# A decoder step on one core: the sample's cache pages laid on 32 partitions each instead of 128

## The chip, the cores and the metric

The kernel runs on one core of one Trainium2 chip. The metric is the device time of one execution in microseconds. The engines are TensorE (PE, with its weight loads as PEld), VectorE (DVE), ScalarE (ACT), GpSimd (POOL) and SyncE (SP). A transfer between device memory and the on-chip memory of 128 partitions is cut into packets, one for each contiguous run, and the packets are moved by the core's 16 DMA engines. Transfers are issued by SP (queue q1 in the profile), by ACT (queue q10) and by POOL (queue q0); each queue keeps its own order.

## The reference

One layer of a hybrid decoder for a prompt of 1024 tokens and a sample of 8 sequences with one new token each. Every token passes an attention with a compressed cache, a retention branch, and a mixer in which each of 8 heads picks 16 of 16384 experts, whose rows of `peer_u` and `peer_v` (4 KB each) are fetched by number. The change touches only the sample's attention over its paged cache:

```
ckv_all = concatenate([cache_ckv[l][page_table].reshape(DB, past_len, KV_LORA), ckv], axis=1)
kr_all  = concatenate([cache_krope[l][page_table].reshape(DB, past_len, QK_ROPE), krope], axis=1)
s = (einsum('bqhc,bkc->bhqk', q_abs, ckv_all)
     + einsum('bqhr,bkr->bhqk', q_pe, kr_all)) * scale
p = softmax(s)
o = einsum('bhqk,bkc->bqhc', p, ckv_all)
```

A page holds 128 tokens. A token is 256 numbers of the latent (1 KB in float32) and 32 numbers of the rotary key (128 bytes). Each of the 8 sequences has 32 pages. Softmax and both sums run over all the tokens of a sequence, so that the order of the tokens is free as long as scores, probabilities and values agree on it.

## The kernel before, in words

The prompt is worked in 8 blocks of 128 tokens, then the sample as a ninth block. Beside each block's "front" (projections, attention, retention) run the "experts" of the block before: POOL gathers rows of 128 tokens at a time (512 KB a gather) into a ring of 9 slots, DVE multiplies the `u` rows with the token, and the `v` rows are added by DVE or, by way of a diagonal made by ACT, by PE. How many expert steps stand between two pieces of the front is fixed at build time, the same on all engines.

The sample's part has two stages that matter here.

- The retention stage (`dve_sample_ret`, `pe_sample`, `sp_sample`). For each of the 8 sequences SP loads a state of 512 KB into one of three buffers, DVE updates it (L2074), PE multiplies with it (L1074), and SP stores it (L684). A buffer is loaded again only when its store has landed (L678, then L652). Between these, on the same queue, SP issues one group of four pages and their rotary keys for each sequence (`load_pages`, L664 and L668). So in SP's queue stand, again and again: load of a state, four pages, four rotary keys, store of a state.
- The attention stage (`pe_sample_attention`, `act_sample_attention`, `dve_sample`). A sequence is 8 groups of four pages. For each group DVE transposes the pages and the keys in blocks of 32 by 32 (L2087, L2088), PE makes the scores with 9 pairs of matmuls (L1107), and a sequence later PE multiplies probabilities and pages (L1141). 16 places hold groups; SP refills a place when PE has used it (L662). From group 8 on the rotary keys are issued by ACT (`load_ropes`, L1623), between its own computing: exponents, the diagonals for the experts (L2254), and the queries of the next sequence (`stage_queries`, L1588 and L1590), which stand behind the loads of a whole sequence in ACT's order.

Each page number is read from the page table into a register (L659, L1617), and each page is a transfer of its own. DVE waits for the 8 transfers of a group together (L2085).

Of the kernel before, what the change touches and what calls it, by code (L numbers as in the profile page):

```python
# [19 lines left out]
ds = bass.ds  # L20
# [76 lines left out]
def program(nc, a, out, const):  # L97
    _, SEQ, D = a["x_prompt"].shape
    NB = a["x_sample"].shape[0]
    _, NPHYS, PAGE, KVL = a["cache_ckv"].shape  # L100
    ROPE = a["cache_krope"].shape[3]
# [67 lines left out]
    for t, part in order:  # L169
        for i, (name, w, c, wd) in enumerate(b for b in stream if b[0] == part):  # L170
            if shared(t, name, i):
                continue
            k = w.shape[0] // P
# [3 lines left out]
    def used_through(t, name, i):  # L177
        return sum(load_at[t, name, i])
# [4 lines left out]
    with ExitStack() as ctx:  # L183
# [3 lines left out]
        def sem(name):  # L187
            return ctx.enter_context(nc.semaphore(name))
# [302 lines left out]
        s_pages = [sem(f"s_pages{i}") for i in range(PAGE_SLOTS)]  # L491
# [130 lines left out]
        def page_at(g):  # L622
            i = g % PAGE_SLOTS
            home, i = ((KV, i) if i < NCH else (wbuf, i - NCH) if i < NCH + 4 else (z, i - NCH - 4) if i < NCH + 6
                       else (xr[T % 2], 0) if i == NCH + 6 else (uk, 0))
            return home[:, i * 4 * KVL:(i + 1) * 4 * KVL]
# [6 lines left out]
        def krope_at(g):  # L633
            i = g % PAGE_SLOTS
            if i >= 14:
                return knat[:, (i - 14) * 4 * ROPE:(i - 13) * 4 * ROPE]
            return KV[:, VAT + i * 4 * ROPE:VAT + (i + 1) * 4 * ROPE]

        def s_state_buf(b):
            at_ = VAT + NPAGES * ROPE + b % 3 * RH * RDV  # L640
            return KV[:, at_:at_ + RH * RDV]

        def sp_sample(sp):

            pv_done.wait(sp, T - 1)
            sp.wait_ge(s_gates, 16)
            DJ.wait_drained(sp, T - 1, "stateU")
            sp.dma_start(out["ret_p"][0, 0].rearrange("h d e -> d h e"),
                         state[:, :].rearrange("p (h e) -> p h e", h=RH)).then_inc(state_out, 16)

            def load_state(b):
                sp.dma_start(s_state_buf(b).rearrange("p (h e) -> p h e", h=RH),  # L652
                             a["state_ret"][0][ds(b, 1)].rearrange("o h d e -> d (o h) e")).then_inc(s_state_in[b % 3], 16)

            sp.wait_ge(table_in, 16)

            def load_pages(g):

                _, numbers = nc.values_load_multi_w_load_instructions(  # L659
                    pages_reg[0:1, 4 * g:4 * g + 4], engines=[mybir.EngineType.SP], min_val=0, max_val=NPHYS - 1)  # L660
                if g >= PAGE_SLOTS:
                    sp.wait_ge(s_pv.sem, g - PAGE_SLOTS + 1)  # L662
                for k, page in enumerate(numbers):
                    sp.dma_start(page_at(g)[:, k * KVL:(k + 1) * KVL],  # L664
                                 a["cache_ckv"][0][ds(page, 1)].rearrange("o p c -> (o p) c")).then_inc(s_pages[g % PAGE_SLOTS], 16)
                if g < NCH:
                    for k, page in enumerate(numbers):
                        sp.dma_start(krope_at(g)[:, k * ROPE:(k + 1) * ROPE],  # L668
                                     a["cache_krope"][0][ds(page, 1)].rearrange("o p c -> (o p) c")).then_inc(s_pages[g % PAGE_SLOTS], 16)

            for b in range(2):
                load_state(b)
            for b in range(NB):
                if b + 2 < NB:

                    s_oret.wait(sp, b - 1)
                    if b >= 1:
                        sp.wait_ge(s_state_stored[(b + 2) % 3], 16 * ((b + 2) // 3))  # L678
                    load_state(b + 2)
                for c in range(NCH):  # L680
                    if c * NB // NCH == b:
                        load_pages(c)
                s_state_new.wait(sp, b)
                sp.dma_start(out["ret_s"][0][b:b + 1].rearrange("o h d e -> d (o h) e"),  # L684
                             s_state_buf(b).rearrange("p (h e) -> p h e", h=RH)).then_inc(s_state_stored[b % 3], 16)
            sp.wait_ge(ckv_stored, 32 * (T + 1))
            s_masked.wait(sp, NB - 1)
            ret_squares.wait(sp, T)
            sp.dma_start(flat, out["ckv_s"][0].rearrange("b s c -> s (b c)")).then_inc(s_flat, 16)
            sp.wait_ge(w_used, used_through(T, "uq", NU - 1))  # L690
            for i in range(3):
                sp.wait_ge(s_state_stored[i], 16 * len(range(i, NB, 3)))
            sp_store_y(sp, T - 2)
            for g in range(NCH, NB * NCH):
                if g == NCH + 6:
                    sp.wait_ge(y_stored, 16 * (T - 1))
                if g == NCH + 7:
                    AS.wait_drained(sp, 0, "qabs")
                load_pages(g)
# [879 lines left out]
        def act_sample_attention(act):  # L1579
            AS.wait_drained(act, 0, "qabs")  # L1580
            act.wait_ge(s_setup, 1)

            def stage_queries(b):
                s_sc_filled.wait(act, b - 2)
                queries = qrep.rearrange("p (k h b) -> p k h b", k=9, h=NH)
                for q in range(4):
                    quarter = slice(32 * q, 32 * (q + 1))
                    nc.scalar.activation(qsc[b % 2].rearrange("p (k q m) -> p k q m", k=8, q=4)[quarter, :, q, 0:NH],  # L1588
                                         queries[quarter, 0:8, :, b], ACT.Copy)
                    last = nc.scalar.activation(qsc_rope[b % 2][quarter, 32 * q:32 * q + NH], queries[quarter, 8, :, b], ACT.Copy)  # L1590
                last.then_inc(s_staged.sem, 1)

            def exponents(b):
                s_nm.wait(act, b)
                s_pt.wait(act, b - 1)
                nc.scalar.activation(WK[:, 0:D], PS[:, scores_at(b):scores_at(b) + 2 * 512], ACT.Exp, bias=nmx[:, 0:1], scale=SCALE,
                                     accum_out=sums[:, 0:1]).then_inc(s_exp.sem, 1)
                s_diff.wait(act, b)
                nc.scalar.activation(pnew4.rearrange("p (j m) -> p j m", j=4), drow.unsqueeze(1).broadcast_to([1, 4, 32]), ACT.Exp,
                                     scale=SCALE).then_inc(s_exp.sem, 1)  # L1600

            def scaled(b):
                s_pv_new.wait(act, b)
                s_weight.wait(act, b)
                nc.scalar.activation(o_sc, bank[6][:, 0:KVL], ACT.Copy, scale=sums[:, 1:2]).then_inc(s_osc.sem, 1)

            def turned_out(b):
                s_ot_filled.wait(act, b)
                nc.scalar.activation(ota.rearrange("p (c b) -> p c b", b=NB)[:, :, b], bank[6][:, 400:400 + 2 * NH],
                                     ACT.Copy).then_inc(s_ota.sem, 1)  # L1610

            act.wait_ge(table_in, 16)

            def load_ropes(g):
                if g >= NB * NCH:
                    return
                _, numbers = nc.values_load_multi_w_load_instructions(  # L1617
                    pages_reg[0:1, 4 * g:4 * g + 4], engines=[mybir.EngineType.Activation], min_val=0, max_val=NPHYS - 1)
                s_turned.wait(act, 0, g - PAGE_SLOTS + 1)
                if g == 14:  # L1620
                    act.wait_ge(ckv_stored, 32 * (T + 1))
                for k, page in enumerate(numbers):
                    act.dma_start(krope_at(g)[:, k * ROPE:(k + 1) * ROPE],  # L1623
                                  a["cache_krope"][0][ds(page, 1)].rearrange("o p c -> (o p) c")).then_inc(s_pages[g % PAGE_SLOTS], 16)

            for i in range(3):
                act.wait_ge(s_state_stored[i], 16 * len(range(i, NB, 3)))
            stage_queries(0)
            for b in range(NB):
                for c in range(NCH):  # L1630
                    load_ropes((b + 1) * NCH + c)
                    if b > 0 and c in (1, 3, 4):
                        {1: exponents, 3: scaled, 4: turned_out}[c](b - 1)
                    if c == NCH - 1 and b + 1 < NB:
                        stage_queries(b + 1)
                    yield "page"
            for stage in (exponents, scaled, turned_out):
                stage(NB - 1)
# [692 lines left out]
PAGE_SLOTS = 16  # L2331
# [76 lines left out]
```

## Time and profile before

| | us |
|---|---|
| median of 3 runs | 4161.53 (4159.66 to 4172.78) |
| the profiled execution's own time | 4134.78 |
| its span | 4133.0 |
| PE busy | 3237.0 (78%) |
| DVE busy | 2704.7 (65%) |
| POOL busy | 2527.7 (61%) |
| ACT busy | 742.9 (18%) |
| mean rate of the DMA engines | 360 GB/s |

The profile is of one execution. All places in time below are microseconds from the start of its span. The sample's retention stage begins near 3456, its attention's first scores stand at 3604, and its last at 3925; what follows is the sample's projections and experts, up to 4133. "Packets" are counted for each queue; a queue's share is the time that its packets took as a share of the time of all 16 DMA engines.

### The profile page before, as it was taken

The numbers are of one execution on the slowest core, as the hardware profiler recorded it, in microseconds if no ns is written. First come the engines' busy times: TensorE is split into PE (matmuls) and PEld (weight loads), VectorE is DVE, ScalarE is ACT, GpSimd is POOL, SyncE is SP. The second block draws the span as 40 slices with busy tenths as digits, with TensorE's granted clock in tenths as the row PEclk, the third lists the DMA queues.
The fourth block names the chain that finished last, engine by engine and source line by source line (L and its number), as shares of the span: only waits on it lengthen the run. The fifth ranks groups of instructions, "written<-read, shape, count | busy, mean of one in ns | idle before, by whom it ended". The sixth has DMA issues, their size and how long they took to land.

```text
span 4133.0 us, 39221 instructions
## 1 busy us (share of the span) xinstructions
PE 3237.0 (78%) x11253; PEld 1588.6 (38%) x11253; DVE 2704.7 (65%) x6214; ACT 742.9 (18%) x2277; POOL 2527.7 (61%) x2069
## 2 busy tenths in 40 slices
PE   7887877876889876877988777877888777599954
PEld 3334333432344332433444233423344333366622
DVE  2156667767777568766886577756875577556554
ACT  2112111220112111211122022211122120111121
POOL 0005766777667767776667677666767677445462
PEclk9998999988999999889999999999999997799987
DMA  5668999999999999999999999999999999999996
GB/s 181 219 219 304 398 393 397 359 395 389 397 375 389 402 402 338 368 399 398 398 367 403 402 380 358 386 401 391 386 384 399 391 371 331 326 311 365 348 356 246
DMA packets 576043, 1489.93 MB, mean 360 GB/s; under 512 B 90267, under 2 KB 147236, under 8 KB 575812
## 3 DMA queue, kind: packets, MB, share of 16 engines
q0 software_dynamic: 297216, 1082.26, 68.3%
q1 hardware_dynamic: 238514, 392.77, 26.5%
q10 hardware_dynamic: 40098, 12.39, 1.3%
q8 instruction: 92, 1.51, 0.2%
q14 instruction: 123, 1.00, 0.1%
HBM read 1477.01 MB, written 10.20 MB: 360 GB/s over the span
## 4 chain that ended last, share of the span: by engine, by line
PE 36%; DMA 25%; POOL 17%; DVE 11%; issue 8%; ACT 3%; ACTq 1%; SPq 0%; POOLq 0%; DVEq 0%
DMA rows<-in_peer_v_dram,pe_id 16%; POOL rows L728 16%; PE PS L1190 12%; PE PS L823 11%; DMA rows<-in_peer_u_dram,pe_id 3%; PE PS L1107 3%; DVE rows L2148 3%; PE PS L832 2%; DMA wbuf<-in_w_out_dram 2%; PE PS L788 1%; DMA wbuf<-in_peer_w_q_dram 1%; DVE xr L2174 1%; PE PS L968 1%; PE PS L948 1%; DMA wbuf<-in_w_in_dram 1%
## 5 line engine op out<-in xcount | busy, mean ns | idle before, releaser
L728 POOL DMA_INDIRECT rows<-in_peer_u_dram,pe_id x1024 | 1259.9, 1230 | 880.0 <-DVE pe_id L1953 297.4
L1190 PE MATMUL PS<-rows,diags 128*128 128x512 f32 x2544 | 1344.0, 660 | 484.0 <-DMA rows<-in_peer_v_dram,pe_id 443.7
L728 POOL DMA_INDIRECT rows<-in_peer_v_dram,pe_id x1024 | 1248.3, 1219 | 671.6 <-DVE dots L2148 377.8
L2148 DVE CUSTOM_DVE_ANT_0 rows<-rows,px 128x1024 f32<-128x1024 f32 x1024 | 1242.0, 1223 | 525.0 <-DMA rows<-in_peer_u_dram,pe_id 520.4
L1190 PEld LDWEIGHTS PS<-rows,diags 128*128 128x128 f32 x2544 | 485.8, 206 | 1132.4 <-issue 979.2
L823 PE MATMUL PS<-wbuf,xt 128*128 128x512 f32 (+1 forms) x1696 | 780.4, 595 | 73.5 <-DMA wbuf<-in_w_in_dram 31.3
L2174 DVE SCALAR_TENSOR_TENSOR xr<-rows,gcoef,xr 128x1024 f32<-128x1024 f32 x388 | 498.3, 1284 | 149.1 <-issue 135.4
L823 PEld LDWEIGHTS PS<-wbuf,xt 128*128 128x128 f32 x1696 | 320.1, 196 | 494.3 <-issue 347.2
L823 PE MATMUL PS<-wbuf,wide 128*128 128x512 f32 (+1 forms) x736 | 341.6, 606 | 35.2 <-ACT wide L1301 14.8
L2254 ACT ACTIVATE diags<-ident,gcoef 128x128 f32<-128x128 f32 x636 | 231.4, 399 | 218.6 <-PE PS L1190 100.6
L823 PEld LDWEIGHTS PS<-wbuf,wide 128*128 128x128 f32 x736 | 143.6, 200 | 215.9 <-issue 162.5
L788 PE MATMUL PS<-ident,WK 128*128 128x128 f32 x572 | 96.0, 311 | 91.3 <-DVE WK L1867 47.7
L832 PE MATMUL PS<-wbuf,KV 128*128 128x512 f32 (+1 forms) x352 | 156.0, 565 | 0.0
L788 PEld LDWEIGHTS PS<-ident,WK 128*128 128x128 f32 x572 | 78.4, 161 | 139.2 <-DVE WK L1867 56.1
L1290 ACT ACTIVATE z<-PS 128x512 f32<-128x512 f32 (+1 forms) x60 | 32.8, 567 | 469.9 <-PE PS L823 210.6
L968 PE MATMUL PS<-KV,WK 128*128 128x64 f32 x576 | 81.9, 290 | 29.9 <-ACT WK L1445 29.9
L1290 ACT ACTIVATE WK<-PS 128x512 f32<-128x512 f32 x42 | 25.1, 597 | 429.9 <-PE PS L823 280.0
L948 PE MATMUL PS<-KV,qt 96*128 96x512 f32 (+3 forms) x192 | 79.6, 525 | 27.3 <-DVE mx L1816 25.7
L832 PEld LDWEIGHTS PS<-wbuf,KV 128*128 128x128 f32 x352 | 65.7, 190 | 77.2 <-issue 77.2
L968 PEld LDWEIGHTS PS<-KV,WK 128*128 128x128 f32 x576 | 73.0, 200 | 45.9 <-ACT WK L1445 40.2
L1440 ACT ACTIVATE WK<-WK,nmx 128x128 f32<-128x128 f32 (+7 forms) x64 | 49.5, 774 | 206.3 <-DVE nmx L1820 206.3
L1859 DVE TENSOR_TENSOR xr<-PS,xr 128x512 f32<-128x512 f32 x16 | 11.1, 692 | 113.8 <-PE PS L823 113.8
(375 smaller groups left out, 2682.0 us busy)
## 6 DMA issues: line engine op xcount, KB each, us to landing
wbuf<-in_w_in_dram SPq DMA_DIRECT2D x274, 512.0 KB, 10.1
wbuf<-in_peer_w_q_dram SPq DMA_DIRECT2D x134, 512.0 KB, 12.1
wbuf<-in_w_ob_dram SPq DMA_DIRECT2D x66, 512.0 KB, 8.5
wbuf<-in_w_out_dram SPq DMA_DIRECT2D x66, 512.0 KB, 11.1
wbuf<-in_w_oa_dram SPq DMA_DIRECT2D x36, 512.0 KB, 8.1
rows<-in_peer_u_dram,pe_id POOLq DMA_INDIRECT x1028, 9.3
rows<-in_peer_v_dram,pe_id POOLq DMA_INDIRECT x1024, 9.3
KV<-in_cache_ckv_dram SPq DMA_DIRECT2D x128, 128.0 KB
```

The source lines that it names most:

```text
L728: pool.indirect_dma_start(row_slot(kind, n), None, a["peer_u" if kind == "u" else "peer_v"][0], bass.IndirectOffsetOnAxis(ap=pe_id[t % 2][ ...
L788: last = nc.tensor.transpose(b[0:m, k * n:(k + 1) * n], src, ident[0:n, 0:n])
L823: last = nc.tensor.matmul(bnk, lhs[:, (k0 + j) * P:(k0 + j + 1) * P], block_w[:, j * wd:(j + 1) * wd], start=(k0 + j == 0), stop=(n == n0 ...
L832: last = nc.tensor.matmul(other, next_lhs(t, k0 + j), block_w[:, j * wd:(j + 1) * wd], start=(k0 + j == 0), stop=(n == n0 + slots - 1 and ...
L948: last = nc.tensor.matmul(DD.bank(tj, "score", h)[:, i:i + w], qt[0:HD, h * P:(h + 1) * P], key_t[0:HD, h, i:i + w], start=True, stop=True)
L968: last = nc.tensor.matmul(bank[6][:, h * VH:(h + 1) * VH], pt[:, k * P:(k + 1) * P], value[:, k, h * VH:(h + 1) * VH], start=(k == 0), sto ...
L1107: last = nc.tensor.matmul(PS[:, at_:at_ + P], qsc[b % 2][:, k * P:(k + 1) * P] if k < 8 else qsc_rope[b % 2], blocks_of[:, k] if k < 8 els ...
L1190: last = nc.tensor.matmul(bank[3 + 4 * c], diag(n), row_slot("v", n)[:, c * 512:(c + 1) * 512], start=start, stop=stop)
L1290: return nc.scalar.activation(dst[:, at_:at_ + wd], b[:, 0:wd], func, scale=scale)
L2148: V.tensor_tensor_reduce(out=row, in0=row, in1=px[:, :], scale=1.0, scalar=0.0, op0=ALU.mult, op1=ALU.add, accum_out=dots[:, at_:at_ + 1]) ...
L2174: V.scalar_tensor_tensor(out=y[:, :], in0=row_slot("v", n), scalar=gcoef[:, g % 2 * TOPK + k:g % 2 * TOPK + k + 1], in1=y[:, :], op0=ALU.m ...
L2254: nc.scalar.activation(diag(n), ident[:, :], ACT.Copy, scale=gcoef[:, g % 2 * TOPK + k:g % 2 * TOPK + k + 1]).then_inc(diag_ready.sem, 1)
```

## The change

Where four pages of a group stood beside each other along the free axis of all 128 partitions (page k in columns k * 256 to (k + 1) * 256, a token to a partition), now page k stands in partitions 32k to 32k + 31, and each partition holds four neighbouring tokens of it in its 1024 columns. The rotary keys are laid in the same way. The tiles, their size, the transposes, the matmuls, the waits and the number and order of all instructions are as before; each transfer names 32 rows of 4 KB in place of 128 rows of 1 KB (keys: 32 rows of 512 bytes in place of 128 of 128 bytes).

```
@@ load_pages, issued by SP @@
                 for k, page in enumerate(numbers):
-                    sp.dma_start(page_at(g)[:, k * KVL:(k + 1) * KVL],
-                                 a["cache_ckv"][0][ds(page, 1)].rearrange("o p c -> (o p) c")).then_inc(s_pages[g % PAGE_SLOTS], 16)
+                    sp.dma_start(page_at(g)[32 * k:32 * (k + 1), :],
+                                 a["cache_ckv"][0][ds(page, 1)].rearrange("o (p s) c -> (o p) (s c)", s=4)).then_inc(s_pages[g % PAGE_SLOTS], 16)
                 if g < NCH:
                     for k, page in enumerate(numbers):
-                        sp.dma_start(krope_at(g)[:, k * ROPE:(k + 1) * ROPE],
-                                     a["cache_krope"][0][ds(page, 1)].rearrange("o p c -> (o p) c")).then_inc(s_pages[g % PAGE_SLOTS], 16)
+                        sp.dma_start(krope_at(g)[32 * k:32 * (k + 1), :],
+                                     a["cache_krope"][0][ds(page, 1)].rearrange("o (p s) c -> (o p) (s c)", s=4)).then_inc(s_pages[g % PAGE_SLOTS], 16)
@@ load_ropes, issued by ACT @@
                 for k, page in enumerate(numbers):
-                    act.dma_start(krope_at(g)[:, k * ROPE:(k + 1) * ROPE],
-                                  a["cache_krope"][0][ds(page, 1)].rearrange("o p c -> (o p) c")).then_inc(s_pages[g % PAGE_SLOTS], 16)
+                    act.dma_start(krope_at(g)[32 * k:32 * (k + 1), :],
+                                  a["cache_krope"][0][ds(page, 1)].rearrange("o (p s) c -> (o p) (s c)", s=4)).then_inc(s_pages[g % PAGE_SLOTS], 16)
```

## Rows read from the trace of the kernel before

**Rows 1.** Stretches: from:to, length, busy us of engines, clock, DMA share, GB/s

```profile
3456.00:3565.00 109.00, 70.48 (x246) 32.55 (x246) 72.15 (x150) 7.55 (x28) 58.46 (x49) 0.76 0.93 327
...
3650.00:3900.00 250.00, 241.98 (x1687) 170.68 (x1686) 159.23 (x295) 41.39 (x137) 124.28 (x110) 0.99 1.02 345
```

**Rows 2.** Waits of PE, 3600 to 3925: us in total, times, longest

```profile
PE PS L1107 <- ACT knat L1590: 6.2, 1, 6.2
...
PE PS L1190 <- DMA rows<-in_peer_v_dram,pe_id: 3.3, 1, 3.3
```

**Rows 3.** Waits of SP, 3650 to 3900

```profile
SPq L664 <- PE PS L1141: 89.2, 6, 31.6
```

**Rows 4.** Waits of POOL, 3650 to 3900

```profile
POOL rows L728 <- DVE dots L2148: 103.8, 26, 11.0
```

**Rows 5.** Chain that ended last, retention stage: start us, us, what

```profile
3494.09 9.18 DMA out_ret_s_dram<-KV
...
3509.89 19.98 DMA out_ret_s_dram<-KV
3529.93 3.94 DMA KV<-in_state_ret_dram
```

**Rows 6.** Waits of DVE, 3456 to 3600

```profile
DVE KV L2074 <- DMA KV<-in_state_ret_dram: 18.2, 3, 15.7
```

**Rows 7.** DMA queues, 3509.9 to 3529.9: packets, MB, share of 16 engines

```profile
q0 software_dynamic: 1813, 6.58, 81.5%
q1 hardware_dynamic: 1666, 1.10, 17.2%
```

**Rows 8.** Order of time on ACT, 3600 to 3650: start us, us, what, count

```profile
3602.66 5.92 ACTq L1623 DMA_DIRECT2D KV<-in_cache_krope_dram  x8
...
3610.47 6.16 ACTq L1623 DMA_DIRECT2D KV<-in_cache_krope_dram  x8
...
3618.22 10.02 ACTq L1623 DMA_DIRECT2D KV<-in_cache_krope_dram  x8
...
3629.83 8.96 ACTq L1623 DMA_DIRECT2D knat<-in_cache_krope_dram  x8
...
3641.19 5.13 ACTq L1623 DMA_DIRECT2D KV<-in_cache_krope_dram  x8
```

**Rows 9.** Order of time on PE, 3590 to 3650: in brackets the idle time before

```profile
3593.45 3.75 PE L1190 MATMUL PS<-rows,diags 128*128 128x512 f32 x4 [7.80 <-DMA rows<-in_peer_v_dram,pe_id]
3600.47 3.65 PE L1190 MATMUL PS<-rows,diags 128*128 128x512 f32 x4 [3.26 <-DMA rows<-in_peer_v_dram,pe_id]
...
3640.68 3.75 PE L1107 MATMUL PS<-KV,state 128*128 128x128 f32 x16 [6.24 <-ACT knat L1590]
...
3644.87 1.98 PE L1107 MATMUL PS<-KV,state 128*128 128x128 f32 x16
```

**Rows 10.** DMA queues, 3600 to 3641

```profile
q0 software_dynamic: 3205, 11.68, 74.8%
q1 hardware_dynamic: 3482, 3.16, 23.1%
q10 hardware_dynamic: 4063, 0.46, 7.9%
```

**Rows 11.** Order of time on SP: store of a state (512 runs), and later pages

```profile
3509.89 0.43 SPq L684 DMA_DIRECT2D out_ret_s_dram<-KV  x1
...
3585.74 12.87 SPq L664 DMA_DIRECT2D wbuf<-in_cache_ckv_dram  x16
```

**Rows 12.** Rate of the DMA engines in 40 equal slices of the span

```profile
GB/s 181 219 219 304 398 393 397 359 395 389 397 375 389 402 402 338 368 399 398 398 367 403 402 380 358 386 401 391 386 384 399 391 371 331 326 311 365 348 356 246
```

**Rows 13.** DMA queues, 3650 to 3900

```profile
q0 software_dynamic: 15552, 56.63, 60.9%
q1 hardware_dynamic: 28148, 26.16, 32.2%
q10 hardware_dynamic: 26496, 3.03, 8.5%
```

## The prediction

> **What bounds the kernel now.** I read the stretches first, because the change touches only 3456 to 3900 of the 4133 us. In the attention stage PE is busy 241.98 of 250 us at a granted clock of 0.99 of full speed [rows 1]. SP waits 89.2 us there for PE to free a place for pages, so pages are loaded as far ahead as they can be [rows 3], and POOL waits 103.8 us for DVE to free a row slot [rows 4]. In the list of PE's waits no page and, after 3604, no expert row appears [rows 2]. So this stage is PE's, although the DMA engines are nearly full: 345 GB/s at a share of 1.02 [rows 1]. Faster page loads buy nothing in it; slower ones may cost.
>
> Before it things are different. From 3456 to 3565 PE is busy 70 of 109 us and DVE 72 [rows 1]. The chain of waits goes there through two stores of a state, 9.18 and 19.98 us from issue to landing, and the load of a state that waits for the second, 3.94 us [rows 5]. DVE stands for that 15.7 us in one piece, of 18.2 in all [rows 6]. 512 KB in 20 us is no transfer's own time: something is ahead of it in its queue. And at 3640.68 PE starts the second sequence 6.24 us late, waiting for ACT's queries [rows 9], while ACT's order of time shows nothing but issues of rotary keys [rows 8].
>
> **How the queues share.** This decides the sign of most terms. While the second store waits, POOL's queue moves 1813 packets (81.5% of 16 x 20 us, or 144 ns each) and SP's 1666 (17.2%, or 33 ns each) [rows 7]. From 3600 to 3641 it is 3205, 3482 and 4063 packets on three queues [rows 10]. The counts are alike where bytes differ twentyfold: full queues take turns by packet. A queue of small packets therefore pays for each the 144 ns of a gathered row that goes first. In an SP queue, one DMA engine finds 4 x 8 page packets of 1 KB, 4 x 8 key packets of 128 bytes and 32 packets of 1 KB of the state: 96, and 96 x (144 + 33) ns = 17.0 us, near the 19.98 seen.
>
> **The change part by part.**
>
> 1. The store and load chain in the retention stage. Pages and keys of a group go from 64 packets on each engine to 8 + 8 = 16. 48 fewer turns at 144 ns are 6.9 us less before the second store lands. Their bytes are unchanged. The first store of the chain lands after 9.18 us in place of 19.98; by that ratio it gains 0.46 x 6.9 = 3.2 us, and the second is issued that much earlier. What comes back: in the old run the gathers had run dry when the next state was loaded in 3.94 us; with no drought its 32 packets take 32 x 177 ns = 5.7 us, 1.8 more. Sum -6.9 - 3.2 + 1.8 = -8.3 us, and I take -8. The wait of 18.2 us [rows 6] is the other end, if it goes whole; 0 is the end on this side, if what is removed ahead of the store is paid at once in late expert rows. Next in line there are the expert rows and SP's own issue time (8 issues for a group), which stays.
>
> 2. ACT's queue. Eight key loads cost ACT 5.13 us when nothing stops them; four batches before took 5.92, 6.16, 10.02 and 8.96 [rows 8]. The excess, 31.06 - 4 x 5.13 = 10.5 us, is the issuing instruction held up by a queue that drains a 9-packet share by turns. With a quarter of the data packets the queue drains faster than ACT can fill it: 2 packets and their turns, 2 x (144 + 33 + 21) ns = 0.4 us by the 21 ns of a q10 packet in the densest row that has one (7.9% of 16 x 41 us over 4063 is 12.8 ns, so 21 is high), or 0.7 us when its SP turns are 4 KB packets of 144 ns, against 5.13 / 8 = 0.64 us per issue. ACT is then ready 10.5 us sooner and PE needs only 6.24 of it. PE's first 16 matmuls after the gap took 3.75 us where the next 16 took 1.98 [rows 9]; without the gap that 1.8 goes too. Sum -8.0 us. Ends: 0, if the hold-up stays, and -10.
>
> 3. Expert rows just before the attention. From 3585.74 SP issues eight groups, 32 pages of 128 KB or 4.2 MB, the first 16 in 12.87 us [rows 11]. Their packets of 4 KB now take as much as a gathered row's in each turn, so that rows come later while pages come sooner. PE waits 7.80 and 3.26 us for `v` rows there [rows 9]; 2 MB of pages moved ahead of them (those first 16) would be 5 us at the 400 GB/s of the fastest slices [rows 12]. I take +3, between 0 and +5.
>
> 4. The attention stage. The same bytes in fewer packets: 1 KB packets took 32.2% of 16 x 250 us / 28148 = 46 ns, so four are 183 ns, and a 3.6 KB packet of q0 took 60.9% of 4000 / 15552 = 157 ns [rows 13], 176 for 4 KB. No gain there. Keys: 12.8 ns a packet, four are 51 ns against an estimated 22 for 512 bytes. Over 26496 / 4 that is 192 engine-us, 12 us of each engine's 250. It is slack and PE does not wait for it: 0 us. The cover is PE's own work; if DMA became the bound, this 12 us would count. Issues stay as they are in number, and their price hardly follows the runs: a store of 512 runs took 0.43 us to issue [rows 11], a key load of 128 no more than 0.64 with all that lies between two of them [rows 8].
>
> 5. Transposes, matmuls and softmax see tiles of the same size: 0. No wait is added.
>
> The sum is -8 - 8 + 3 = -13 us. The profiled execution took 4134.78 us (a span of 4133.0 and 1.8 around it), so 4121.8 for it. The median of the runs shown stands 26.8 above that execution; I carry the difference over: 4161.5 - 13 = 4148.5.
>
> **A rule that speaks against it.** All rows agree only on destinations of 128 partitions. The Trainium skill, page "SBUF — State Buffer", section "Door 1: The DMA port swizzle (why [64,N] ≈ [32,N])", says that partitions 0 to 31 reach only 8 of 16 write ports, and gives 189 GB/s there against 328 over all 128, for 1 MiB. No row here shows a transfer of 32 partitions. By that rule a page would move at little over half the rate; what follows is the second rival.
>
> **The rivals.**
>
> First: the turns do not shrink with the packets, because several short packets of one transfer are taken in one turn. For it: the number of transfers stays. Against it: the near equal counts on queues with 4 KB, 1 KB and 128 byte packets [rows 7, 10]. Then term 1 is 0, ACT's hold-up shrinks only in part, and the rows keep their place: -5, or 4156.5.
> The Trainium skill, page "DMA: Bandwidth & Descriptors", section "Queues, rings and completion order", has it so: an engine drains a packet of some 9 to 17 descriptors from one ring before it switches. The counts of rows 7 and 10 would have to be alike by chance.
>
> Second, slower: a destination of 32 partitions is written at half the rate. The place is the attention stage, whose DMA engines are at 1.02 [rows 1]. Groups 16 to 63 are loaded there, 192 pages or 25 MB; at 345 GB/s they take 73 us of the 250 and would take 73 more. The keys give 12 back [rows 13]. Up to 400 GB/s [rows 12] there are 250 x (1 - 345/400) = 34 us of slack, so PE would wait 27 us. Term 1 is lost, since the turns that it saves are spent on slower pages, term 3 with it, and term 2 stays with half of its 8: +23, or 4184.5. It decides from the point where DMA needs over 34 us more than now, a page at about 1.6 times its present time. Against it: pages of a group alternate over all partitions, and gathers run beside them.
>
> Third: the 8 and the 8 are gained, but the rows that follow are late, since the gathers were as near to the bound as the stores (4 KB packets of pages take turns from them in every stage); PE and DVE wait for rows instead: 0 to -4, say 4159.5.
>
> **How the numbers follow.** Forecast 0.42, first rival 0.16, second 0.20, third 0.22. The likeliest case has its own range by the bounds of terms 1 to 3: 4161.5 - 28 to 4161.5 + 5; its likely part is 4134 to 4156. The whole range goes from 4130 to 4180, which leaves out the far end of the second rival and of term 1. A measurement of this kernel tells 0.3% (12.5 us) from no change. The forecast is at that bound, and I give two thirds of it and a little of the others to faster: 0.40; slower is most of the second rival, 0.19; the rest, 0.41, is no change that can be told.
>
> **What would show it.** Step 1: the two stores land in about 6 and 12 us and DVE's wait for a state falls from 18.2 to about 10. Step 2: every batch of eight key loads takes about 5.1 us and PE no longer waits for L1590. Step 3: PE's waits for `v` rows before 3604 grow from 11 to about 14. Step 4: q1 has about 28148 - 3/4 x 24576 = 9700 packets in the attention stage, and PE stays over 0.96 busy. The prediction is wrong if the packets of pages take well over 183 ns each and PE or DVE wait for rows or pages after 3650; or if the stores land as late as before, with fewer packets ahead of them.

## The result, and the profile after

The changed kernel takes 4200.14 us (median of 5 runs, 4192.04 to 4211.61); the kernel before took 4161.22 in the same comparison. The ratio is 1.0092, with a 95% interval of 1.0071 to 1.0112: 0.9% slower, 39 us. The forecast was 4148.5 us, faster, with a range up to 4180.

Where the time went is seen if the sample's part is cut at three places that every kernel has: SP's issue of line 594 (the start), the first score (L1107), and the first matmul of L1171 behind the attention. "Before, again" is a second profile of the unchanged sample code (from the kernel with the probe, below); it shows how much one profile differs from the next.

| profile | start to first score | attention | from there to the end |
|---|---|---|---|
| before | 147.7 | 323.8 | 205.2 |
| before, again | 150.7 | 336.7 | 207.5 |
| changed | 153.5 | 370.5 | 208.1 |

So the attention stage, where I expected nothing, lost 34 to 47 us, and the retention stage, where I expected a gain, lost 3 to 6. The two profiled executions of before and after stand 64 us apart where the medians stand 39 apart, and 8 us of that lie ahead of the start, where the change does nothing: a few microseconds between single profiles prove nothing.

The attention stage before and after, and the stretch of [rows 1] after (from:to, length, busy us of PE, PEld, DVE, ACT, POOL, then clock, DMA share, GB/s):

```profile
3604.00:3927.80 323.80, 305.82 (x2090) 216.99 (x2089) 196.43 (x360) 51.04 (x168) 154.97 (x138) 0.97 1.01 343
...
3618.00:3988.50 370.50, 320.12 (x2089) 222.72 (x2087) 196.50 (x360) 50.96 (x168) 154.35 (x137) 0.95 1.01 297
...
3650.00:3900.00 250.00, 217.99 (x1408) 153.32 (x1407) 137.08 (x255) 35.11 (x115) 107.18 (x96) 0.95 1.00 283
```

From 3650 to 3900 the DMA engines are as busy as before (1.00 against 1.02) and move 283 GB/s where they moved 345: full engines that carry less. PE is busy 218 of 250 us where it was busy 242. Over the whole stage PE's idle time grows from 18 to 50 us. The other 14 us of the 47 are PE's own: the same matmuls take 320 us in place of 306 (312 in "before, again"), at a mean granted clock of 0.95 against 0.97. In the 14 us before the first score, where PE was busy only 3.9 us, that clock was 0.50. The queues from 3650 to 3900, as in [rows 13]:

```profile
q0 software_dynamic: 13034, 47.46, 62.2%
q1 hardware_dynamic: 7474, 20.44, 32.0%
q10 hardware_dynamic: 7549, 2.59, 5.5%
```

Two things are to be read here. The gathered rows (q0), which the change does not touch, now take 62.2% of 16 x 250 us over 13034 packets = 191 ns each, where they took 157. The keys of the whole stage come in 10752 packets where they came in 32256, a third: each of the 224 loads counts 48 in place of 144, which is its 32 or 128 rows and 16 more. What PE waits for in the attention stage, 3618.0 to 3988.5, the answer to [rows 2] (us in total, times, longest):

```profile
PE PS L1190 <- DMA rows<-in_peer_v_dram,pe_id: 24.8, 10, 4.7
PE PS L1107 <- issue: 8.1, 4, 3.5
PE PS L1190 <- issue: 7.5, 2, 5.0
PE PS L1190 <- ACT diags L2254: 4.5, 2, 3.7
```

Before, no expert row stood in this list (the 3.3 us of [rows 2] end before the first score); now they lead it with ten waits, 24.8 us in all. The pages themselves are not late: SP still waits for PE to free places (L664 in SP's waits, the answer to [rows 3]), now longer, because PE is later.

```profile
SPq L664 <- PE PS L1141: 116.6, 5, 46.9
```

ACT's batches of eight key loads, as in [rows 8], are short up to the second sequence, and PE's wait for ACT's queries before it is gone. The waits at the other starts are not: L1107 stands above with 8.1 us, where it had 6.2 + 5.2 before.

```profile
3614.94 5.03 ACTq L1623 DMA_DIRECT2D KV<-in_cache_krope_dram  x8
3621.85 4.93 ACTq L1623 DMA_DIRECT2D KV<-in_cache_krope_dram  x8
3628.37 4.92 ACTq L1623 DMA_DIRECT2D KV<-in_cache_krope_dram  x8
3634.87 4.98 ACTq L1623 DMA_DIRECT2D knat<-in_cache_krope_dram  x8
```

And PE just before and among the first scores, as in [rows 9]:

```profile
3600.53 3.75 PE L1190 MATMUL PS<-rows,diags 128*128 128x512 f32 x4 [6.80 <-DMA rows<-in_peer_v_dram,pe_id]
3614.42 3.75 PE L1190 MATMUL PS<-rows,diags 128*128 128x512 f32 x4 [10.13 <-DMA rows<-in_peer_v_dram,pe_id]
...
3656.26 1.95 PE L1107 MATMUL PS<-KV,state 128*128 128x128 f32 x16
```

The last of these rows is the start of the second sequence: no gap before it, and 1.95 us for 16 matmuls where they took 3.75. In the retention stage the chain of stores goes (SP's order of time; the load behind each store is issued when the store has landed):

```profile
3501.62 0.42 SPq L684 DMA_DIRECT2D out_ret_s_dram<-KV  x1
3512.75 0.40 SPq L652 DMA_DIRECT2D KV<-in_state_ret_dram  x1
...
3520.57 0.40 SPq L684 DMA_DIRECT2D out_ret_s_dram<-KV  x1
3533.59 0.40 SPq L652 DMA_DIRECT2D KV<-in_state_ret_dram  x1
```

11.1 and 13.0 us in place of 9.18 and 19.98 [rows 5]: 24.1 in sum against 29.2, where I had forecast 10 less. But two more profiles of unchanged loads have 28.2 ("before, again") and 20.5 us (e8 below) for the same two stores, so that no gain can be read here. DVE's waits before L2074, against 18.2 us in [rows 6], are 17.1 in two lines:

```profile
DVE KV L2074 <- DMA KV<-in_state_ret_dram: 12.8, 1, 12.8
...
DVE KV L2074 <- issue: 4.3, 1, 4.3
```

### The profile page after: what moved, and what is told of

The parts are those of the page before. It is cut to its first block, busy times and chain, and to the rows that moved or that the text cites. A ratio compares the mean times of both kernels' runs of the same rounds, so it can differ in the third digit from the quotient of the medians.

```text
span 4196.6 us, 39221 instructions
## 1 busy us (share of the span) xinstructions
PE 3253.5 (78%) x11253; PEld 1596.1 (38%) x11253; DVE 2705.9 (64%) x6214; ACT 743.4 (18%) x2277; POOL 2515.3 (60%) x2069
## 4 chain that ended last, share of the span: by engine, by line
PE 31%; DMA 27%; POOL 15%; issue 12%; DVE 10%; ACT 3%; another core or an unknown queue 1%; ACTq 0%; DVEq 0%; SPq 0%; POOLq 0%
DMA rows<-in_peer_v_dram,pe_id 19%; POOL rows L728 15%; PE PS L823 10%; PE PS L1190 10%; DMA rows<-in_peer_u_dram,pe_id 4%; DVE rows L2148 2%; PE PS L832 2%; DMA wbuf<-in_peer_w_q_dram 2%; PE PS L1107 2%; PE PS L788 1%; DMA wbuf<-in_w_in_dram 1%; DVE xr L2174 1%; PE PS L968 1%; PE PS L885 1%
## 5 line engine op out<-in xcount | busy, mean ns | idle before, releaser
L823 PE MATMUL PS<-wbuf,xt 128*128 128x512 f32 (+1 forms) x1696 | 780.4, 595 | 82.1 <-DMA wbuf<-in_w_in_dram 31.1
L823 PE MATMUL PS<-wbuf,wide 128*128 128x512 f32 (+1 forms) x736 | 337.5, 599 | 31.1 <-ACT wide L1301 14.7
L1816 DVE CUSTOM_DVE_ANT_0 WK<-PS,WK 128x128 f32<-128x128 f32 (+7 forms) x64 | 48.2, 754 | 60.8 <-PE PS L948 60.7
```

The lines of the kernel that those rows point to most:

```text
L823: last = nc.tensor.matmul(bnk, lhs[:, (k0 + j) * P:(k0 + j + 1) * P], block_w[:, j * wd:(j + 1) * wd], start=(k0 + j == 0), stop=(n == n0 ...
```

## The experiments

Two theories of the loss. A: a transfer whose destination is 32 neighbouring partitions is written slowly, and holds up what runs beside it. B: the place costs nothing, but packets of 4 KB take long turns between the gathered rows. All ratios are to the kernel before on the same chip, whose median there was 4153.29 us (e1 to e4), 4157.51 (m1, e5 to e7) or 4162.25 (e8 to e11); the expectations in microseconds are meant for 4161, so the ratios are what to compare. A hunk stands for all three places of the load (SP's pages, SP's keys, ACT's keys) where nothing else is said.

**e1: the same rows, four partitions apart.**

```
-sp.dma_start(page_at(g)[32 * k:32 * (k + 1), :],
+sp.dma_start(page_at(g)[k:P:4, :],
...
```

> The same 32 rows of 4 KB (keys 512 bytes) in each transfer as in the changed kernel, but the rows of page k go to partitions k, k + 4, k + 8 and so on, over all 128, in place of 32k to 32k + 31. The changed kernel moved 283 GB/s at a DMA share of 1.00 between 3650 and 3900 where the kernel before moved 345 at 1.02. Theory A (a destination of 32 neighbouring partitions is written more slowly than one spread over all 128): the loss of 39 us goes, the attention stage is back near 323 us, its DMA share falls under 1 at some 340 GB/s, and the gains forecast for the retention stage and for ACT's queue (up to 16 us) can show: 4135 to 4165. Theory B (a 4 KB page packet takes as long a turn as a gathered row's packet, so rows come late): packets and turns are those of the changed kernel, so it stays at 4190 to 4210.

Measured: 4171.33 us, ratio 1.0041 (1.0022 to 1.0060). That is between what the two theories expected. More than half of the loss is gone, which B, as it stood, does not allow, since packets and turns are the same; the rest A did not expect. In its attention stage, 356.2 us long (3604.3 to 3960.5), the DMA engines are no longer full:

```profile
q0 software_dynamic: 20395, 74.24, 58.7%
q1 hardware_dynamic: 12219, 31.60, 24.9%
q10 hardware_dynamic: 10752, 3.68, 4.2%
```

The sum is 88%, a gathered row's packet takes 164 ns, and PE waits for no expert row. It waits for something else now:

```profile
PE PS L1107 <- issue: 24.8, 6, 7.4
```

These waits are at the starts of sequences, where PE needs the queries that ACT stages behind its key loads. The issuing instructions (ns min/median/max) have become dearer. First the changed kernel, ACT's and SP's:

```profile
L1623 ACTq DMA_DIRECT2D KV<-in_cache_krope_dram x192: 3/322/1534, 3614.9 to 3925.5; - x192
L664 SPq DMA_DIRECT2D KV<-in_cache_ckv_dram x128: 3/316/721, 3472.4 to 3893.8; - x128
```

and e1:

```profile
L1623 ACTq DMA_DIRECT2D KV<-in_cache_krope_dram x192: 170/489/1363, 3603.2 to 3899.9; - x192
L664 SPq DMA_DIRECT2D KV<-in_cache_ckv_dram x128: 3/472/927, 3460.2 to 3873.0; - x128
```

A transfer that steps over partitions costs its issuer 0.16 us more. Over the 32 key loads of a sequence that is 5 us of ACT.

**e2: only the pages.** The keys' hunks are taken back; scores then add pages and keys of different tokens, and the work is the same.

> Only the pages lie on 32 partitions each; the rotary keys are loaded as in the kernel before, so that keys and pages of a score belong to different tokens (the sums are not the reference's; the work is the same). Both theories lay the loss on the pages, whose bytes are 8 times those of the keys: A and B expect 4195 to 4215, a little above the changed kernel, since the keys' small packets stay and ACT is held up in its issues again.

Measured: 4226.55 us, 1.0177 (1.0143 to 1.0211). The loss is the pages', and it is above the changed kernel and above what was expected. Its engines are as slow as the changed kernel's (a gathered packet takes 184 ns), but PE waits for something else: 31.1 us without a named releaser before L1107, 13.8 for ACT's L1599, and only 10.3 for expert rows. With 144 packets to a key load, ACT is held up in its issues: they take over 200 us of its stage in sum, some 125 in the changed kernel and some 140 before (the rows of L1623 in ACT's order of time, added up).

**e3: only the keys.** The pages' hunk is taken back, and again keys and pages of a score are of different tokens.

> Only the rotary keys lie on 32 partitions each, the pages as in the kernel before (again the keys belong to other tokens than the pages). Theories A and B: the keys are 4 MB, so that their place costs nearly nothing, and a quarter of their packets frees ACT's queue: the wait of 6.24 us before the second sequence and the slower matmuls behind it go, -8 us, and the stores in the retention stage have 24 packets less ahead of them on each engine, -3 to -5 us: 4149 to 4155. If the forecast's terms 1 and 2 are not real: 4161.

Measured: 4144.47 us, 0.9977 (0.9956 to 0.9998), a gain of some 9 us, as expected for this part. ACT's second to fourth batch of eight take 5.0 to 5.1 us. DVE's wait for a state is lower than in the three profiles of unchanged loads, which have 18.2 [rows 6], 19.1 ("before, again") and 14.1 (e8):

```profile
DVE KV L2074 <- DMA KV<-in_state_ret_dram: 8.5, 2, 7.7
```

Even so its retention stage is 147.4 us, no shorter than the 147.7 before. The two ratios of e2 and e3 also say that the keys' part of the change is worth some 0.8% of the time beside slow pages (1.0177 against 1.0092) and 0.2% beside fast ones.

**e4: the halves in turn.**

```
-for k, page in enumerate(numbers):
+for k, page in ((k, numbers[k]) for k in (0, 2, 1, 3)):
...
```

> The changed kernel with the four pages (and keys) of a group issued in the order 0, 2, 1, 3, so that two transfers behind each other go to different halves of the partitions; nothing else differs. Theory A, if a slow write path blocks only until the other half's turn: part of the 39 us comes back, 4175 to 4195. Theory A, if each transfer is slow by itself whatever stands beside it: 4200. Theory B: 4200.

Measured: 4197.58 us, 1.0101 (1.0068 to 1.0134). Nothing comes back. The order of the transfers in the queue doesn't help.

**m1: the loads alone.** Before anything else on SP, with no other transfer under way, nine batches of 2 MB, each waited for:

```
+for kind in ("wide", "near", "turn", "lower", "step4", "step2", "four", "wide", "near"):
+    for i in range(4 if kind == "four" else 16):
+        g, k = divmod(i, 4)
+        ...                     # near: tile[32 * k:32 * (k + 1), g * D:(g + 1) * D]
+        sp.dma_start(dst, src).then_inc(probe, 16)
+        sent += 16
+    sp.wait_ge(probe, sent)
```

> The disputed cost by itself: the kernel before, with nine batches of cache loads of 2 MB put at its very start, when no other transfer runs; SP waits for each batch before the next. In order: (1) 16 pages on 128 partitions in 1 KB runs, (2) 16 pages on 32 neighbouring partitions each in 4 KB runs, pages 0 to 3 on the four quarters in turn, (3) the same in the order of quarters 0, 2, 1, 3, (4) all 16 pages on the two lower quarters, (5) 32 partitions at a step of 4, (6) 32 partitions at a step of 2 inside one half, (7) four transfers of four pages each on 128 partitions in 4 KB runs, (8) as 1, (9) as 2. Theory A (the place of the 32 partitions sets the rate): 1, 5, 7 and 8 run at 330 to 400 GB/s (or at SP's issue rate, 128 KB in some 0.4 us), and 2, 4 and 9 clearly below, near 200; 6 like 2. Theory B (the place costs nothing, only the turns beside gathers do): all batches of 4 KB runs are as fast as batch 1 or faster.

Measured: the middle stretch of batches 1 (18 to 26 us), 2 (30 to 37), 4 (51 to 59), 5 (63 to 72), 6 (75 to 84) and 7 (87 to 92), from the DMA view of these stretches (the table has 3, 41 to 47, 8, 95 to 102, and 9, 105 to 113, from the same view):

```profile
q1 hardware_dynamic: 2208, 2.01, 85.5%
...
DMA packets 602, 1.64 MB, mean 234 GB/s; under 512 B 202, under 2 KB 202, under 8 KB 602
q1 hardware_dynamic: 602, 1.64, 103.1%
...
DMA packets 616, 1.68 MB, mean 210 GB/s; under 512 B 206, under 2 KB 206, under 8 KB 616
q1 hardware_dynamic: 616, 1.68, 104.0%
...
q1 hardware_dynamic: 655, 1.78, 63.6%
...
q1 hardware_dynamic: 673, 1.84, 68.0%
...
DMA packets 500, 1.82 MB, mean 365 GB/s; under 512 B 55, under 2 KB 55, under 8 KB 500
q1 hardware_dynamic: 500, 1.82, 96.2%
```

SP issues a load of 128 KB every 0.47 us in batch 1 and every 0.64 us in batches 5 and 6, and that sets their rates: 252, 199 and 205 GB/s. So the number to compare is what a megabyte costs the engines: share x 16 x length / MB.

| batch | destination | runs | engines | engine-us per MB |
|---|---|---|---|---|
| 1 (and 8) | all 128 | 1 KB | 0.86 busy | 54 (53) |
| 2 (and 9) | 32 neighbours, quarters in turn | 4 KB | full | 70 (68) |
| 3 | 32 neighbours, halves in turn | 4 KB | 0.91 busy | 57 |
| 4 | 32 neighbours, lower half only | 4 KB | full | 79 |
| 5 | 32 at a step of 4 | 4 KB | 0.64 busy | 51 |
| 6 | 32 at a step of 2 in a half | 4 KB | 0.68 busy | 53 |
| 7 | all 128, 512 KB a load | 4 KB | 0.96 busy | 42 |

Batches 5 and 6 do not tell a half from the whole: where the engines are idle a third of the time, both cost about the same. Among the batches that fill the engines, 32 neighbours cost 70 to 79 and all 128 partitions 42, although batch 7 also has fewer and larger loads. With full engines the lower half takes 210 GB/s, and quarters in turn 234. This agrees with theory A; B, by which every batch of 4 KB runs would be as fast as batch 1, fails for batches 2, 4 and 9. The expectation "6 like 2" did not come. Batch 3 was cheaper alone, though in the kernel (e4) that order gave nothing.

The whole kernel took 4258.4 us in its one run, the probe's 97 us included.

The Trainium skill, page "SBUF — State Buffer", section "Door 1: The DMA port swizzle (why [64,N] ≈ [32,N])", gives 189 GB/s for 1 MiB on partitions 0 to 31, 196 on 0 to 63, and some 218 as the limit of both. The 210 here, on partitions 0 to 63, lie between.

**e6: pages four apart, keys on neighbours** (of different tokens in a score, as in e2).

> Pages at a step of 4 partitions, as in e1; keys on 32 neighbouring partitions, as in the changed kernel (keys and pages of a score belong to different tokens; the work is the same). In e1 the DMA engines had room (share 0.88) but each stepped key load took ACT 0.49 us to issue where the changed kernel's took 0.32, and PE waited 24.8 us at the starts of sequences. Theory A with the issue price as what is left of e1: ACT's price goes, the waits at the starts fall to 8 us or so, and the time is 10 to 17 us under e1's, 0.998 to 1.001 of the kernel before. Theory B (turns of 4 KB packets): it stays with e1 at 1.004 or above.

Measured: 4168.4 us, 1.0021 (1.0006 to 1.0036). PE's waits before L1107 fall from 24.8 to 14.2 us and the attention stage from 356.2 to 339.7. So ACT's price was part of PE's waits in e1. In the time it doesn't show clearly: the intervals of e1 and e6 overlap, and the kernel is above the 0.998 to 1.001 that was expected.

**e7: e1 with the queries early.**

```
+if c == 2 and b + 1 < NB:
+    stage_queries(b + 1)
 load_ropes((b + 1) * NCH + c)
 ...
-if c == NCH - 1 and b + 1 < NB:
-    stage_queries(b + 1)
```

> e1 with ACT staging the next sequence's queries before its key loads of c = 2 and not behind those of c = 7. If ACT's issues ahead of the queries make PE's waits in e1 (24.8 us before L1107), they go and the time falls by 15 to 25 us below e1, to 0.993 to 0.999 of the kernel before. If the waits are for pages that land late, moving the queries changes nothing: 1.004.

Measured: 4169.89 us, 1.0029 (1.0012 to 1.0046), against e1's 1.0041. The waits before L1107 do go:

```profile
PE PS L1107 <- issue: 1.7, 2, 1.3
```

That shows what they were. But the time hardly follows: PE now waits 8.8 us for ACT's L1599, 4.9 and 2.9 before the maxima and 3.4 for DVE's reciprocal. ACT, later by its issues, is late at the next step. What was expected here was missed.

**e5: two apart, inside one half.**

```
-sp.dma_start(page_at(g)[32 * k:32 * (k + 1), :],
+sp.dma_start(page_at(g)[64 * (k // 2) + k % 2:64 * (k // 2 + 1):2, :],
...
```

> The changed kernel with the rows of pages 0 and 1 interleaved on partitions 0 to 63 and those of 2 and 3 on 64 to 127: 32 partitions at a step of 2 inside one half. Theory A in the form that each half of the partitions has its own write paths: the DMA engines are as slow as in the changed kernel and the stepped issue costs ACT as in e1 on top: 1.010 to 1.016. Theory A in the form that neighbouring partitions are what collides: as e1, 1.004.

Measured: 4223.9 us, 1.0153 (1.0119 to 1.0186). Attention 379.4 us, DMA share 1.00 at 291 GB/s. The issues cost what they cost in e1 (467 and 488 ns), so the step is paid in both and the half makes the difference: 32 rows that stay in 0 to 63 or in 64 to 127 are slow beside the gathers even when they are not neighbours, and 32 rows that reach over both are not (e1).

**e10: neighbours with short runs.**

```
+sp.dma_start(page_at(g)[32 * k:32 * (k + 1), :].rearrange("p (s c) -> p s c", s=4),
+             a["cache_ckv"][0][ds(page, 1)].rearrange("o (s p) c -> (o p) s c", s=4))
...
```

> Place and packet size taken apart, first half: page k lies on partitions 32k to 32k + 31 as in the changed kernel, but in the packets of the kernel before: a partition takes the tokens p, p + 32, p + 64, p + 96, so that every run is one token, 1 KB (keys 128 bytes). The result is the reference's. If the place makes the loss, it stays, and with small packets of keys as in e2: 1.010 to 1.018 of the kernel before. If the 4 KB packets make it (long turns beside the gathered rows), the loss goes: 0.998 to 1.003.

Measured: 4200.72 us, 1.0088 (1.0060 to 1.0116): the changed kernel's loss with the packets of the kernel before, and a little under the 1.010 to 1.018 expected. Its queues in the attention stage (3616.1 to 3989.8):

```profile
q0 software_dynamic: 20466, 74.49, 62.2%
q1 hardware_dynamic: 33060, 32.33, 33.2%
```

Here the packets of q1 are like those before in number and size and can be compared directly: 33.2% of 16 x 373.7 us over 33060 is 60 ns, where the kernel before has 48 in the same stage. The gathered rows' packets take 182 ns against 156. But the slow engines reach PE by another way than in the changed kernel. Its wait for expert rows is 1.3 us; it waits for the queries:

```profile
PE PS L1107 <- issue: 18.2, 4, 5.5
PE PS L1107 <- ACT knat L1590: 12.8, 1, 12.8
```

Two batches of eight key loads before the second sequence take ACT 15.67 and 12.34 us, and its issues over 200 us of the stage, as in e2. So with many small key packets the slow engines hold up ACT, and with few of them they make the expert rows late. Why e2 lost twice as much as e10 is not shown: they differ in the pages' runs and in the keys' place.

**e11: four apart with short runs**, the same with `page_at(g)[k:P:4, :]`.

> Second half: partitions k, k + 4, ... as in e1, with runs of 1 KB (keys 128 bytes) as in the kernel before. e1 is at 1.0041 and e6, the same pages with quickly issued keys, at 1.0021. If what is left there is the 4 KB packets' long turns, short runs take it away on the pages' side: 0.998 to 1.002. If it is the stepped issue (SP 0.47 us in place of 0.33), it stays: 1.003 to 1.007, a little above e1 since ACT's queue holds up its issues again.

Measured: 4191.92 us, 1.0064 (1.0043 to 1.0084).

```profile
q0 software_dynamic: 20359, 74.09, 57.6%
q1 hardware_dynamic: 32972, 32.30, 26.9%
```

Quick engines again (q1 at 47 ns, q0 at 164), and a time no better than e1's; the intervals of e10 and e11 overlap. The stepped destination with four runs to a partition takes SP 0.60 us to issue:

```profile
L664 SPq DMA_DIRECT2D KV<-in_cache_ckv_dram x128: 3/602/1392, 3475.2 to 3906.9; - x128
```

Short runs thus take nothing away from what e1 left. PE waits 27.4 + 5.6 us before L1107; whether the dearer issues or the small key packets make that, e11 does not separate.

**e9: the changed kernel with the queries early** (the edit of e7).

> The changed kernel with the queries staged early. If its loss is the slow write of 32 neighbouring partitions, PE goes on waiting for expert rows and the time stays at 1.007 to 1.010. If a good part of the loss is ACT being late (10.1 us of its waits name ACT or nothing): 1.004 or below.

Measured: 4205.41 us, 1.0093 (1.0057 to 1.0129): what ACT was late with at the starts of sequences has no part in the loss that can be seen. PE's first wait stays the expert rows:

```profile
PE PS L1190 <- DMA rows<-in_peer_v_dram,pe_id: 27.2, 10, 5.1
```

**e8: the kernel before with the queries early** (the edit of e7).

> The kernel before with ACT staging the next sequence's queries before its key loads of c = 2 and not behind those of c = 7; the loads are as before. The starts of sequences, where PE waited 6.2 + 5.2 us (11.5 + 1.6 in the second profile of the same code), lose these waits and the slow matmuls behind them: 0.995 to 0.999 of the kernel before. This is term 2 of the forecast taken without the change. If other waits take their place (as e7 against e1, -0.1% where -0.5% was expected): 0.999 to 1.001.

Measured: 4152.15 us against 4162.25, 0.9974 (0.9954 to 0.9994). It leaves the computation and the layout of the kernel before as they are, and is faster than both kernels, by a little. No wait before L1107 is among its longest; the first is

```profile
PE PS L1125 <- DVE mx L2098: 4.9, 2, 4.3
```

**All attention stages side by side.** For each profile the cost of a megabyte on q1, and of a packet on q0 (nearly all gathered rows): share x 16 x length over the megabytes or the packets. The stages are cut as above.

| place of a page | profiles | q1, engine-us per MB | q0, ns a packet | ratios |
|---|---|---|---|---|
| inside one half | changed, e2, e4, e5, e9, e10 | 58 to 61 | 181 to 187 | 1.0088 to 1.0177 |
| all 128, 1 KB runs | before (twice), e3, e8, e11 | 48 to 49 | 156 to 164 | 0.9974 to 1.0064 |
| all 128, 4 KB runs, step of 4 | e1, e6, e7 | 44 to 45 | 160 to 164 | 1.0021 to 1.0041 |

The first row does not touch the other two, whatever the runs, the order, the step or the keys. That the second row has full engines too (0.97 to 1.00 in the two profiles of before and in e8) shows that the difference is not one of load.

## Why the prediction was wrong

The step that failed is term 4, "no gain there ... 0 us", with the sentence that placed the rule against the change below the forecast: the place of the destination has a price, and it measured +34 to +47 us in the attention stage. I had the mechanism as the second rival and gave it 0.20 and 4184.5 us.

The rival's parts were wrong too, in both directions. It let the pages' own bytes take 73 us more; q1's share x length grew from 98 to 117 us, 19 more. It priced the gathered rows at nothing: 20600 of their packets went from 156 to 184 ns, 28 ns x 20600 / 16 = 36 us of each engine. The keys gave 7 back where I had 12. And it allowed 34 us of slack, from a rate of 400 GB/s, though the share of 1.02 in [rows 1] said that the engines had none. PE then waits for expert rows, and runs part of its matmuls at a lower granted clock. My sign of being wrong has come: at 60 engine-us per MB a run of 4 KB on q1 costs 247 ns, where the same bytes took 199 before (49 per MB) and I had 183, and PE waits for rows after 3650.

What I held against that rival, that the pages of a group alternate over all partitions and gathers run beside them, is refuted by the changed kernel itself, whose gathered packets took 191 ns, and by e4 (1.0101).

Point by point:

- Term 1, -8 us: not shown. The two stores landed in 24.1 us in place of 29.2, but profiles of unchanged loads have 20.5 to 29.2, and DVE's wait for states spreads there from 14.1 to 19.1. With the keys' change alone (e3) it is 8.5 and the stores take 19.8, which fits a gain of a few microseconds; yet no part of it reached the end of the stage (147.4 us in e3), as in my third rival. The reasoning by turns has better support, see the first rival.
- Term 2, -8 us: right in kind, its size not shown. The batches before the second sequence took 4.9 to 5.0 us and there was no wait before it, but at the other starts PE still waits: before L1107, for ACT or without a named releaser, 8.1 us in the changed kernel and 9.6 in e3, against 11.4 and 13.1 in the two profiles of the old code. Taken alone in two ways the term is worth -0.23% with the keys (e3, which holds term 1 too) and -0.26% without any change of layout (e8), some 10 us, with intervals that reach from nearly 0 to 0.46%. The second profile of the old code had 1.6 us at the place where the first had 6.2, and 11.5 where the first had 5.2, at the other starts: the wait was real, its place in one profile was chance. A small slip beside it: 2 x (144 + 144 + 21) ns is 0.6 us, not 0.7.
- Term 3, +3 us: the two waits for `v` rows were 6.80 and 10.13 us against 7.80 and 3.26, +6. Over the whole retention stage these waits are 20.6 us against 20.2, and e7, with the pages four apart, has 19.1: neither the turns of 4 KB that I named nor the place is shown as a cause.
- Term 4, 0: +34 to +47 us in the profiles.
- The first rival (turns by transfer). The near equal counts of [rows 7] and [rows 10] did not speak against it: a gather, a page and a key load had 144 packets each before, so whole transfers in turn would give equal counts too. The changed kernel's profile decides it. Its page has 48 packets and a gather still 144, and from 3605 to 3617, with full engines, the queues moved

```profile
q0 software_dynamic: 505, 1.87, 58.5%
q1 hardware_dynamic: 505, 1.39, 44.6%
```

  one for one, where turns by transfer would give three to one; in e4 from 3610 to 3624 it is 611 and 607. So the turns count packets and not transfers, and the rival is refuted; whether a turn is one packet or a fixed few is not shown.

What stays open: with pages four apart the engines have room (e1, e6, e7, 88 to 91% busy) and yet the time is 0.2 to 0.4% above the kernel before. The dearer issue is shown (0.47 against 0.33 us) and e6 points to it, but e7, which took one of its consequences away, moved the time by only 0.1%, within its interval. No run separated SP's price from ACT's.

## What to carry to other kernels

Fewer and larger packets were no gain here, because the destination then lay in one half of the partitions. Read the rate beside the DMA share: full engines at a lower rate are a reason to look at where transfers are written. The price fell on the transfers beside them as well, so look for it in the waits for data that was not touched. Here a share of 1.0 was no slack, although higher rates stood in other stretches. Before a layout is changed to relieve an issuing engine, try moving what waits behind its issues: here that alone gave 0.26% (0.06 to 0.46).

## What the runs showed of the hardware

- 32 rows inside one half of the partitions, neighbours or two apart, cost 58 to 61 engine-us per MB beside the gathers; 32 rows four apart over all 128 cost 44 to 48, and 128 rows 48 to 49. Alone, the lower half takes 210 GB/s with full engines.
- What shares the engines slows down with them: gathered packets to 128 partitions took 181 to 187 ns beside pages in one half, and 156 to 164 beside pages over all 128.
- Between two queues with work the engines' turns count packets, not transfers: 505 and 505 packets in 12 us, where the transfers of one queue had 144 packets and those of the other 48.
- Stepped destinations cost the issuer more: 316 to 472 ns on SP and 322 to 489 on ACT with one run to a partition. With four runs to a partition it is 602 and 610 at a step of 4, and 317 and 330 on neighbours.
- Neighbours in 32 rows of one run are a little cheaper to issue than 128 rows, 316 against 333 ns.
